# The end of a feed-forward block on one Trainium2 core: the order in which p is split, the last squares are summed and the first embedding tiles are evicted

## The reference

```python
for i in range(DEPTH):
    ...
    h = h + rmsnorm(y, norm_g[i, 1])
    h = h + rmsnorm(swiglu(rmsnorm(h, norm_g[i, 2]), w_gate[i], w_up[i], w_down[i]), norm_g[i, 3])
    h = h + jax.nn.sigmoid(h @ w_ple_gate[i]) * (p[i] @ w_ple[i])
```

## Time and profile before

| what | value |
|---|---|
| median of 3 runs | 3272.09 us (3270.9 to 3272.9) |
| the profiled execution's own time | 3276.35 us |
| its span, first to last instruction | 3274.7 us |
| TensorE matmuls busy (PE) | 96% |
| TensorE weight loads busy (PEld) | 91% |
| VectorE busy (DVE) | 48% |
| ScalarE busy (ACT) | 28% |
| GpSimd busy (POOL) | 8% |
| mean granted TensorE clock | 0.988 |

### The profile page before, as it was taken

The page is one execution under the profiler, slowest core; times in us unless marked ns, Lnnn a source line. Parts: engine busy times, 40 slices in busy tenths (PEclk is TensorE's granted clock), DMA queues, the critical chain, the costliest instruction groups (busy, mean ns, idle before and its releaser), DMA issues.

```text
span 3274.7 us, 52954 instructions
## 1 busy us (share of the span) xinstructions
PE 3145.5 (96%) x20580; PEld 2989.1 (91%) x20580; DVE 1563.5 (48%) x2681; ACT 907.2 (28%) x1640; POOL 266.7 (8%) x319
## 2 busy tenths in 40 slices
PE   7999999999999999999999998989899999999999
PEld 6999989999999998999987775559899999999989
DVE  5443365444445446543335555542744444444462
ACT  3111242111111116422235553333411111111252
POOL 1000010000000001000025551110100000000011
PEclk9999999999999999999999999999999999999999
DMA  2111111111111111113227766961111111111112
GB/s 89 41 43 45 47 33 46 46 46 46 42 43 46 46 59 39 40 46 120 68 60 158 134 122 226 344 243 44 39 46 40 46 40 45 46 46 40 59 43 70
DMA packets 234070, 239.17 MB, mean 73 GB/s; under 512 B 18805, under 2 KB 191861, under 8 KB 233858
## 3 DMA queue, kind: packets, MB, share of 16 engines
q1 hardware_dynamic: 209842, 156.26, 16.3%
q0 software_dynamic: 24016, 79.77, 8.3%
HBM read 201.11 MB, written 18.10 MB: 67 GB/s over the span
## 4 chain that ended last, share of the span: by engine, by line
PE 89%; DVE 5%; ACT 3%; issue 2%; DMA 1%; POOL 1%; DVEq 0%; ACTq 0%; POOLq 0%
PE psum L2040 20%; PE psum L2042 20%; PE psum L2041 20%; PE psum L2066 5%; PE psum L2060 4%; PE psum L2061 4%; PE psum L2527 2%; PE psum L2572 2%; PE psum L2511 2%; PE psum L2496 1%; PE psum L2591 1%; PE psum L2621 1%; PE psum L2497 1%; DVE xs_lo L1529 1%; DVE xs_lo L1743 1%
## 5 line engine op out<-in xcount | busy, mean ns | idle before, releaser
L2040 PE MATMUL psum<-xs_hi,w_hi 128*128 128x384 f32 (+1 forms) x2784 | 915.6, 329 | 15.3 <-issue 9.7
L2042 PE MATMUL psum<-xs_hi,w_lo 128*128 128x384 f32 (+1 forms) x2784 | 911.0, 327 | 0.0
L2041 PE MATMUL psum<-xs_lo,w_hi 128*128 128x384 f32 (+1 forms) x2784 | 910.4, 327 | 0.0
L2040 PEld LDWEIGHTS psum<-xs_hi,w_hi 128*128 128x128 f32 x2784 | 525.1, 189 | 19.3 <-issue 10.8
L2041 PEld LDWEIGHTS psum<-xs_lo,w_hi 128*128 128x128 f32 x2784 | 525.2, 189 | 0.0
L2042 PEld LDWEIGHTS psum<-xs_hi,w_lo 128*128 128x128 f32 x2784 | 524.9, 189 | 0.0
L778 ACT ACTIVATE w_hi<-raw 128x1024 fp32r<-128x1024 f32 x192 | 202.1, 1053 | 538.3 <-DVEq L1325 527.6
L1659 DVE TENSOR_TENSOR y<-y,psum 128x384 f32<-128x384 f32 x528 | 268.9, 529 | 169.0 <-PE psum L2042 169.0
L2042 PE MATMUL psum<-hid_hi,w_lo 128*128 128x384 f32 (+1 forms) x1056 | 346.0, 328 | 0.0
L2040 PE MATMUL psum<-hid_hi,w_hi 128*128 128x384 f32 (+1 forms) x1056 | 345.6, 327 | 0.0
L2041 PE MATMUL psum<-hid_lo,w_hi 128*128 128x384 f32 (+1 forms) x1056 | 345.1, 327 | 0.0
(11 more groups left out here) (300 smaller groups left out, 3897.5 us busy)
## 6 DMA issues: line engine op xcount, KB each, us to landing
kpage<-in_cache_k SPq DMA_DIRECT2D x64, 512.0 KB, 7.1
v_page<-in_cache_v POOLq DMA_DIRECT2D x64, 512.0 KB, 5.5
raw<-in_w_gate SPq DMA_DIRECT2D x44, 512.0 KB, 3.7
raw<-in_w_up SPq DMA_DIRECT2D x44, 512.0 KB, 3.7
raw<-in_w_down SPq DMA_DIRECT2D x44, 512.0 KB, 3.6
raw<-in_w_in SPq DMA_DIRECT2D x24, 512.0 KB, 3.8
raw<-in_w_ple_gate SPq DMA_DIRECT2D x16, 512.0 KB, 4.0
k_hh<-kT_scratch POOLq DMA_DIRECT2D x32, 256.0 KB, 6.5
```

Of the source, the lines that this page charges most:

```text
L2040: M(out, wh, xh, start=first, stop=False)
L2041: M(out, wh, xl, start=False, stop=False)
L2042: return M(out, wl, xh, start=False, stop=last)
```

## The change

Four things. (1) ScalarE makes its half of p's group m - 1 ahead of block m's square instead of behind square and gain, and VectorE splits group m - 1 behind the adds of block m instead of group m - 2. (2) GpSimd sums only blocks 1 to 5; the squares of blocks 6 and 7 are both added by VectorE, tile by tile, and the counts of the semaphores follow. (3) ScalarE keeps the third tile's row behind the first two evictions of the embedding instead of ahead of all, and the evictions around the two halves of tile 0's `xs_hi` are divided 5, 2 and 3 in place of 8, 3 and 1 (the two ahead not counted). (4) VectorE makes `xs_lo` of tile 0 ahead of the release of the first w_ple slab and of `lo(n0)`, instead of behind both.

```diff
-PSQ0 = {"n_ffn0": (0, 0), "n_kv": (7, 6), "n_ffn1": (15, 13)}
+PSQ0 = {"n_ffn0": (0, 0), "n_kv": (7, 5), "n_ffn1": (15, 12)}
@@ GpSimd, ffn
-                for m in range(1, C - 1):
+                for m in range(1, C - 2):
@@ ScalarE, last_down
                     for m in range(C - 1):
+                        if 1 <= m <= PGRPS:
+                            p_high(m - 1)
                         block_squares(f"n_ffn{layer}", y, m, acc_free, ACCS + NT * (b0 + 124 + m + 1))
                         if m < C - 2:
                             gained(m)
-                        if 1 <= m <= PGRPS:
-                            p_high(m - 1)
...
                     last_gained(2)
-                    keep_row(q + 2)
+
+                def last_row():
+
+                    keep_row(TOKS * layer + 3 * NT - 1)
@@ ScalarE, ple
                 first = [(m, t) for m in range(4) for t in range(NT)]
+                for m, t in first[:2]:
+                    embedded(m, t)
+                last_row()
                 hi(n0 - 1)
-                for m, t in first[:8]:
+                for m, t in first[2:7]:
                     embedded(m, t)
                 high(0, 0)
-                for m, t in first[8:11]:
+                for m, t in first[7:9]:
                     embedded(m, t)
                 high(0, 1)
-                embedded(*first[11])
+                for m, t in first[9:]:
+                    embedded(m, t)
                 hi(n0)
@@ VectorE, ffn
-                def last_sum(t):
-
-                    t0, n = TILES[t]
-                    dve.wait_ge(last_squared, NT * layer + t + 1)
-                    if t == 0:
-                        dve.wait_ge(psq_added, PSQ0[name_n][1] + C - 2)
-                    V.tensor_tensor(ssum[:, t0:t0 + n], ssum[:, t0:t0 + n], psq[1][:, t0:t0 + n], ALU.add)\
+                def last_sum(t, m):
+
+                    (t0, n), (squared, summed) = TILES[t], PSQ0[name_n]
+                    if m == C - 2:
+                        dve.wait_ge(psq_ready, squared + C - 1)
+                        dve.wait_ge(psq_added, summed + C - 3)
+                    else:
+                        dve.wait_ge(last_squared, NT * layer + t + 1)
+                        dve.wait_ge(last_summed, 2 * NT * layer + 2 * t + 1)
+                    V.tensor_tensor(ssum[:, t0:t0 + n], ssum[:, t0:t0 + n], psq[m % 2][:, t0:t0 + n], ALU.add)\
                         .then_inc(last_summed, 1)
@@ VectorE, last_down
-                        if 2 <= m:
-                            p_low(m - 2)
+                        if 1 <= m <= PGRPS:
+                            p_low(m - 1)
                         if m == 5:
                             lo(slab + 2)
                     down_added(blk, C - 1, 0)
+                    last_sum(0, C - 2)
                     down_added(blk, C - 1, 1)
-                    last_sum(0)
+                    last_sum(0, C - 1)
+                    last_sum(1, C - 2)
                     down_added(blk, C - 1, 2)
-                    last_sum(1)
+                    last_sum(1, C - 1)
                     inverse_dev(q)
-                    last_sum(2)
+                    last_sum(2, C - 2)
+                    last_sum(2, C - 1)
                     inverse_dev(q + 1)
@@ VectorE, ple
                 scaled(1, 0)
                 scaled(1, 1)
+                low(0)
                 released(emb_item(layer, 4, 0))
                 lo(n0)
-                low(0)
                 added(1, 0)
@@ TensorE, ple
-                    pe.wait_ge(last_summed, NT * layer + t + 1)
+                    pe.wait_ge(last_summed, 2 * NT * layer + 2 * t + 2)
```

More of the change, by code:

```diff
@@ L1058, in ffn, with ple @@
                 last_down(n0 + 64)
-            def ple(layer):
+                return last_row
+            def ple(layer, last_row):
                 n0, b0 = SLAB0[f"pg{layer}"], BLK0[f"pg{layer}"]
@@ L1144, in ple @@
                     block_squares("n_kv", h, C - 1, ple_added, NT * C)
-            ffn(0)
-            ple(0)
+            ple(0, ffn(0))
             hi_run(SLAB0["k"] + 1, 1, ROW_KV)
@@ L1290, in _ @@
             joint("o", y, psq_att, ROW_G + 5, ROW_G + 6, SLAB0["ffn1"])
-            ffn(1)
-            ple(1)
+            ple(1, ffn(1))
         @block.vector
```

## The result

| | before | after |
|---|---|---|
| median of 5 runs of each, same chip | 3272.56 us (3270.9 to 3277.03) | 3257.65 us (3254.47 to 3257.95) |
| ratio, 95% interval | | 0.995 (0.9936 to 0.9965) |
| profiled execution (span) | 3276.35 (3274.7) | 3257.65 (3256.0) |
| mean granted TensorE clock | 0.988 | 0.990 |

The change is faster by 14.9 us (11.5 to 20.9), which is 0.5%.

A forecast was written before the change was run, and what follows sets the result against it. TensorE, taken as busy nearly throughout at 2.4 GHz, bounds the kernel, so only its idle time can be gained. Terms -4.4 - 0.8 - 0.2 + 1.0 - 1.0 give -5.4 us a layer, -10.8 in both: 3261.3 us, range 3259.0 to 3265.3.

The forecast's parts named there:

- Step 1: Before p's transposes: splitting p one block sooner removes all three TensorE waits, -4.4 us a layer.
- Step 2: Before the first token sums: VectorE adding the last two squares makes the sums ready sooner, -0.8 us a layer.
- Step 3: Token rows and evictions: the 0.9 us wait stays, two earlier evictions free TensorE's bank, -0.2 us a layer.
- Step 4: At the gate: earlier xs_lo of tile 0 adds a weight wait, +1.0, and removes two xs_lo waits, -1.0 a layer.
- Rival (c): At the gate: no wait, because xs_hi ends a microsecond sooner; -6.4 us a layer, 3259.3 us; chance 0.05.
- no idle ahead of the transposes: Sign that the forecast is right: no TensorE idle time before L2308 in either layer.
- the single L2066 wait: Sign at the gate: only one TensorE wait for xs_lo, of about 1 us, is left.
- the wait for w_lo: Sign before tile 0 of the gate: a new TensorE wait of about 1 us for VectorE's w_lo.
- (a): First token sums stay late because ScalarE falls further behind in blocks 4 and 5; -4.6 a layer, 3262.9 us; chance 0.11.
- (b): Gate weights come late, a wait of +3.1 us; -3.3 us a layer, 3265.5 us; chance 0.06.
- (d): None of p's wait goes because it sits on something besides VectorE's split; -1.0 us a layer, 3270.1 us; chance 0.03.
- (e): Slower: xs_hi's second half ends as late as now, delaying gate weights; +1.9 us a layer, 3275.9 us; chance 0.03.

The follow-up runs named there:

- e1: Kernel before with only p's split moved one block sooner, both halves; 3266.66 us against 3269.31 for before, ratio .9983.
- experiment 7: Changed kernel with ten unused 128-column matmuls on TensorE, in layer 0 only (3240.09 us) or layer 1 only (3255.69 us).
- e3: Changed kernel with VectorE's release of the first w_ple slab held until xs_lo of tile 0 is written; 3261.29 us against 3269.31 for before.
- the second series: Changed kernel untouched, run again beside the kernel before on another chip; 3257.99 us against 3268.26, 10.3 us less.
- e6: Changed kernel with the sums as before: GpSimd adds block 6's squares, VectorE only block 7's; 3265.57 us against 3273.26 for before.
- e5: Changed kernel with the old order of third row, evictions and xs_hi halves on ScalarE; 3259.50 us against 3269.31 for before.
- e11: Kernel before with p split one block sooner, plus ten unused 384-column matmuls ahead of the first token sums, both layers; 3247.97 us against 3273.26.
- e12: Changed kernel with ten unused 128-column matmuls in layer 0 alone, ahead of layer 1's feed-forward loop; 3240.09 us against 3270.76 for before.
- e13: Changed kernel plus ten layer 0 matmuls, xs_lo of tile 2 before its release, third reciprocal between scalings, tile 0's xs_lo behind lo(n0); 3238.18 us.
- e15: Kernel before with ten unused 128-column matmuls in layer 0, before the first token sums; 3257.04 us against 3268.26, ratio .9967.
- e14: Changed kernel with ten unused 128-column matmuls in layer 1 alone, behind its feed-forward loop; 3255.69 us against 3268.26 for before.

## Why the prediction was wrong

The sign, the place and most terms held; the sum was too small.

- **Step 1, p:** -4.4 forecast, -4.35 measured. That its whole saving reaches the end depended on something unsaid: alone it yields nothing (e1), since the earlier arrival makes a longer wait and that wait lowers the clock. "Only the sums at the end do" wait for ScalarE was right, and was priced only in idle time. The premise was wrong: the prediction read the page's top digits as a clock at its 2.4 GHz level throughout, and concluded that a change can gain only what TensorE idles. A digit is the mean of 82 us, and the mean granted clock of 0.988 already says that it is lower in places: 0.74 over the 13 us shown in experiment 7, for one.
- **Step 2, last squares:** -0.8 forecast, -1.04 measured; the wait is 0.3, where about 0.5 was awaited. GpSimd's add of block 5 after the change is again the lengthened one:

```profile
1238.06 2.54 POOL L608 TENSOR_TENSOR ssum<-ssum,psq 128x1088 f32<-128x1088 f32 x1 [1.70 <-ACT psq L796]
...
1241.41 2.78 POOL L608 TENSOR_TENSOR ssum<-ssum,psq 128x1088 f32<-128x1088 f32 x1 [0.81 <-ACT psq L796]
```

  VectorE's weight split ran from 1240.57 to 1241.79, 0.38 of it beside the add, which took 0.24 longer:

```profile
1240.57 1.22 DVE L1315 TENSOR_TENSOR w_lo<-raw,w_hi 128x1024 fp32r<-128x1024 f32 x1
```

  By the rule that was cited (the Trainium skill, page "SBUF — State Buffer", section "Who interferes with whom") the trace agrees in direction, both times with less than the overlap (0.24 of 0.38, 0.39 of 0.51).
- **Step 3:** the 0.9 us wait stayed, 7.20 from sums to rows in both; -0.2 forecast, -0.16 measured.
- **Step 4, the step that failed:** "ScalarE's gate-weight split waits for that release", made behind xs_lo, was priced at +1.0. Measured: 0. The order in the list was taken for the order in which things take effect; the release came 2.5 us before xs_lo's end, and holding it back costs 1.23 (e3). The 1.0 for the L2066 waits was mis-sized too: 1.32, which the rows already said (0.2 and 1.1), where 1.0 was taken from a working by starts.
- **Sum:** -4.35 - 1.04 - 0.16 + 0 - 1.32 = -6.87 a layer, 13.6 measured in both, for 10.8. Rival (c), given 0.05, had the sum without a gate wait at 6.4 a layer, but for a reason that did not occur: xs_hi, which it had a microsecond sooner, was whole 39.44 us after the first transposes, where the forecast's 1263.1 makes 39.64. Of the rest, 14.9 against 13.6 lies inside the interval, and the second series lies on the other side, so how near the median came to the stages' sum is partly luck.

Of the signs that the prediction named, no idle ahead of the transposes came true (0.2 us is left in one place), and so did the single L2066 wait; the wait for w_lo did not. Rivals (a), (b), (d) and (e) were not seen in the changed kernel, though the mechanisms of (a) and (b) are real: without part 2 the sums are late (e6), without part 3 xs_hi is (e5). Two readings in the rivals were off: "two evictions less" before each half in (b) is one less before the first half and two before the second, counted from the first, or three and four, counted from the third row; and (b)'s own time, 3265.5, lies outside the range that is said to take in most of it.

## What to carry to other kernels

Parts of a reordering aren't additive: 4.4 us saved ahead of the next wait were worth 0 alone and 4.05 in company, depending on who is late next and whether that wait also lowers TensorE's clock. So price a longer wait by the time of the dense matmuls behind it at half clock as well. Don't count on a wait and a release standing behind the data work ahead of them in VectorE's list, unless a semaphore ties them to its end; other engines' lists were not tried. When a profile moves by more than the stages that were edited, measure the stages on their own, hold the rest against the granted clock, and repeat the series on another chip.

## What the runs showed of the hardware that was not expected

- VectorE's release took effect at 1261.9, 2.5 us before the end of the instruction ahead of it (1264.44).
- An idle stretch of 2.1 us on TensorE before a dense one was followed by a granted clock of 0.50 for some 10 us, in three of four cases (both layers of e1, one of e6), and cost 3.7 to 3.9 us; with the same stretch filled it stayed at 1.00.
- Twenty instructions ahead of a loop of TensorE brought the time outside the stages down from between 3121 and 3132 to between 3104 and 3108, in four kernels of four (e11, e12, e13, e15), with the loop's "issue" waits at 0.5 us in place of 8.7 to 12.1 and no fall of the clock in the loop; behind the loop they didn't (e14). With the packets of the instruction queue at 144 or 145 in three and 172 in the fourth, their number is not the cause.
